# Squares added over chunks on VectorE, and memory keys and values made ahead of their root

## The reference

```
def _rmsnorm(x, g):
    y = x * rsqrt(mean(x * x, axis=-1, keepdims=True) + RMS_EPS)
    return y * g

def _mem_kv(mem, mem_norm_g, w_mem_k, w_mem_v):     # mem (1, 256, 1024)
    m = _rmsnorm(mem, mem_norm_g)
    k = (m @ w_mem_k).reshape(bsz, N_MEM, XA_HEADS, XA_HEAD_DIM)    # 4 heads of 128
    v = (m @ w_mem_v).reshape(bsz, N_MEM, XA_HEADS, XA_HEAD_DIM)
    return k, v

n = _rmsnorm(h, norm1_g)
z = n @ w_in + b_in          # u_s5 | conv_glu_in | q_mem | gate_logits
```

## Time and profile before

| what | value |
|---|---|
| time, median of 3 runs | 1924.89 us (1924.7 to 1926.11) |
| the profiled execution | 1929.2 us |
| its span, first to last instruction | 1927.3 us |
| busy share of the span: PE, DVE, POOL, ACT | 79%, 67%, 33%, 27% |
| HBM read | 665.79 MB |
| mean granted TensorE clock | 0.882 |

### The profile page before, as it was taken

One profiled execution on the slowest core, in us unless ns is written; L12 is line 12 of the kernel. 1 busy time (PEld: TensorE's weight loads), 2 busy tenths in 40 slices (PEclk: granted clock), 3 DMA queues, 4 the chain that ended last, 5 costly groups with the idle time before them and its releaser, 6 DMA issues.

```text
span 1927.3 us, 22321 instructions
## 1 busy us (share of the span) xinstructions
PE 1518.3 (79%) x7779; PEld 788.7 (41%) x7779; DVE 1298.6 (67%) x3346; ACT 526.8 (27%) x1278; POOL 642.6 (33%) x605
## 2 busy tenths in 40 slices
PE   8999999799878998988888889656555776655557
PEld 7888887686433443433333434211111111111113
DVE  5998673327766766676677666776777777777755
ACT  3121142104334343343223233322222121222212
POOL 0020030003444333434344434443434444443442
PEclk9989899899989999999997999777787797777778
DMA  5443463558999999999999999999999999999997
GB/s 211 143 88 110 164 156 113 184 191 326 418 418 385 418 418 418 417 417 414 419 409 409 419 420 420 405 422 417 415 422 418 407 402 422 421 422 422 415 421 285
DMA packets 112706, 675.45 MB, mean 350 GB/s; under 512 B 12784, under 2 KB 15296, under 8 KB 42576
## 3 DMA queue, kind: packets, MB, share of 16 engines
q0 software_dynamic: 80816, 577.23, 73.5%
q1 hardware_dynamic: 31216, 95.87, 14.0%
q10 hardware_dynamic: 560, 0.92, 0.2%
HBM read 665.79 MB, written 6.21 MB: 349 GB/s over the span
## 4 chain that ended last, share of the span: by engine, by line
PE 41%; DMA 41%; issue 8%; DVE 5%; POOL 2%; ACT 2%; ACTq 0%; SPq 0%; POOLq 0%; DVEq 0%
DMA upper<-in_peer_uv,upper 21%; DMA lower<-in_peer_uv,upper 19%; PE pair L1191 11%; PE pair L669 7%; PE pair L680 6%; PE pair L1037 5%; PE pair L783 2%; PE pair L1186 2%; DVE upper L2112 2%; PE pair L983 1%; POOL upper L645 1%; ACT upper L1590 1%; DVE lower L2112 1%; POOL lower L645 1%; PE pair L714 1%
## 5 line engine op out<-in xcount | busy, mean ns | idle before, releaser
L1191 PE MATMUL pair<-upper 64*64 64x512 f32 x2368 | 378.7, 750 | 210.4 <-ACT upper L1590 210.3
L645 POOL DMA_INDIRECT upper<-in_peer_uv,upper x324 | 359.0, 1108 | 504.9 <-PE pair L1191 410.6
L645 POOL DMA_INDIRECT lower<-in_peer_uv,upper x220 | 246.7, 1122 | 487.9 <-PE pair L1191 283.0
L1191 PE MATMUL pair<-lower,upper 64*64 64x512 f32 x1600 | 265.0, 772 | 132.7 <-ACT upper L1590 132.6
L2112 DVE CUSTOM_DVE_ANT_0 upper<-upper 128x1024 f32<-128x1024 f32 x172 | 210.8, 1226 | 123.7 <-DMA upper<-in_peer_uv,upper 123.6
L2112 DVE CUSTOM_DVE_ANT_0 upper<-upper,lower 128x1024 f32<-128x1024 f32 x152 | 186.2, 1225 | 129.8 <-DMA upper<-in_peer_uv,upper 129.4
L1191 PEld LDWEIGHTS pair<-upper 64*64 64x64 f32 x2368 | 89.4, 163 | 406.0 <-ACT upper L1590 279.6
L1590 ACT ACTIVATE upper<-upper 128x64 f32<-128x64 f32 (+2 forms) x543 | 155.4, 338 | 307.4 <-DVE upper L2128 304.9
L1398 ACT ACTIVATE upper<-upper 128x4 f32<-128x4 f32 (+1 forms) x141 | 41.9, 297 | 640.8 <-DVE upper L2112 640.8
L1037 PE MATMUL pair<-lower 128*128 128x288 f32 x704 | 212.5, 432 | 4.2 <-ACT upper L1448 4.2
L2112 DVE CUSTOM_DVE_ANT_0 lower<-lower,upper 128x1024 f32<-128x1024 f32 x116 | 142.1, 1225 | 87.5 <-DMA lower<-in_peer_uv,upper 87.4
(11 more groups left out here) (425 smaller groups left out, 1788.5 us busy)
## 6 DMA issues: line engine op xcount, KB each, us to landing
lower<-in_w_in SPq DMA_DIRECT2D x64, 512.0 KB, 4.8
lower<-in_peer_q SPq DMA_DIRECT2D x28, 512.0 KB, 8.0
lower<-in_proj SPq DMA_DIRECT2D x48, 256.0 KB, 7.2
lower<-in_w_out SPq DMA_DIRECT2D x16, 512.0 KB, 4.7
upper<-in_peer_uv,upper POOLq DMA_INDIRECT x324, 12.4
upper<-in_cache_k SPq DMA_DIRECT2D x8, 512.0 KB, 4.5
upper<-in_cache_v SPq DMA_DIRECT2D x8, 512.0 KB, 4.4
lower<-in_peer_uv,upper POOLq DMA_INDIRECT x220, 12.5
```

The source lines that it names most:

```text
L645: pool.indirect_dma_start(row(g), None, a["peer_uv"], bass.IndirectOffsetOnAxis(ap=idx[:, n % 8, j:j + 1], axis=0)).then_inc(row_in[g % RI ...
L1191: mm = pe.matmul(acc[put, r, :], d[own, 0:64], v[own, h * 512:(h + 1) * 512], start=begun, stop=ended)
```

## The change

The sums of squares move. ScalarE squares as before, but VectorE adds the eight squared chunks into the first, memory then tokens, and counts `sums_ok`; TensorE sums over the partitions with one product by ones per half of the tokens, and one for the memory. A second small product with the operands exchanged gives the memory's sum per memory token as a column (`mcol`), beside the row `mr`.

Keys and values no longer wait for the memory's root. VectorE multiplies the memory by its gain alone, and TensorE begins with the four key blocks. The reciprocal root is multiplied in afterwards: into the keys by VectorE (`kT` times `mr`, four instructions, counted by `key_step`), into the values by ScalarE's copy with a scale per partition (`mcol`), two instructions in place of one. In `JOBS` the keys stand ahead of the two sums, and the tokens' sum ahead of the memory's. On VectorE the token norm comes first, then the reciprocals for the memory and the keys' products, then the S5 discretisation as before. SP loads the constants second, tokens behind the first key block, and the S5 pack behind the second value block.

The diff, without the two definitions of semaphores and `mcol` and without the two places (GpSimd's store of the keys, TensorE ahead of the attention) that now wait for `key_step` instead of the keys' eviction:

```diff
@@ -67,7 +67,7 @@
 
 GATES = [f"G{q}.{b}" for q in range(KD) for b in range(3)]
 PRODUCTS = [f"P{q}.{b}" for q in range(KD) for b in (0, 2)] + [f"P{q}.1" for q in range(KD)]
-JOBS = (["ssm", "ssx"] + [f"k{c}" for c in range(4)] + ["v"]
+JOBS = ([f"k{c}" for c in range(4)] + ["ssx", "ssm", "v"]
         + [f"u{c}" for c in range(4)]
         + ["ag0", "ai0", "ag1", "ai1", "T"] + [f"ET{b}" for b in range(4)]
         + ["ag2", "ai2", "z00", "z01", "z02", "ag3", "z10", "z11", "ai3", "q0", "q1", "q2", "q3"]
...
@@ -460,9 +462,7 @@
         @block.sync
         def _(sp):
             sp.dma_start(memT, a["mem_t"]).then_inc(mem_in, 16)
-            sp.dma_start(nT, a["x_t"]).then_inc(x_in, 16)
             sp.dma_start(const, a["consts"]).then_inc(consts_in, 16)
-            sp.dma_start(s5p, a["s5_pack"]).then_inc(s5_in, 16)
 
             def load(name, src, k=KD):
                 s, n = LOAD[name]
...
@@ -484,8 +484,12 @@
 
             for j in range(4):
                 load(f"k{j}", a["w_mem_k"][j])
+                if j == 0:
+                    sp.dma_start(nT, a["x_t"]).then_inc(x_in, 16)
             for j in range(4):
                 load(f"v{j}", a["w_mem_v"][j])
+                if j == 1:
+                    sp.dma_start(s5p, a["s5_pack"]).then_inc(s5_in, 16)
             sp.dma_start(h0.rearrange("p a b c -> p (a b c)"), a["h0"]).then_inc(h0_in, 16)
             for j in range(4):
                 load(f"u{j}", a["w_in"][j])
...
@@ -572,7 +576,7 @@
             pool.affine_select(out=ident, in_=ident, compare_op=ALU.not_equal, fill=1.0, base=0,
                                pattern=[[-1, P]], channel_multiplier=1).then_inc(made, 1)
             pool.memset(ones, 1.0).then_inc(made, 1)
-            filled(pool, "ssm")
+            pool.wait_ge(sums_ok, 2)
             pool.memset(Tm[:, 0:L - 1], 0.0).then_inc(t_zero, 1)
             filled(pool, "v")
             for j in range(HALF):
...
@@ -692,19 +696,6 @@
 
 
             pe.wait_ge(made, 2)
-            ps = begin("ssm")
-            for k in range(KD):
-                pe.wait_ge(msq_ok, k + 1)
-                mm = pe.matmul(ps[:, 0, 0:MEM], ones, msq[:, k, :], start=(k == 0), stop=(k == KD - 1))
-            mm.then_inc(full[0], 1)
-            ps = begin("ssx")
-            for k in range(KD):
-                pe.wait_ge(xsq_ok, k + 1)
-                for h in range(2):
-                    mm = pe.matmul(ps[:, h, 0:HT], ones, xsq[:, k, h * HT:(h + 1) * HT],
-                                   start=(k == 0), stop=(k == KD - 1))
-            mm.then_inc(full[1], 1)
-
             for j in range(4):
                 w = loaded(f"k{j}")
                 ps = begin(f"k{j}")
...
@@ -713,6 +704,16 @@
                         pe.wait_ge(m_ok, k + 1)
                     mm = pe.matmul(ps[:, 0, 0:MEM], w[:, k, :], memT[:, k, :], start=(k == 0), stop=(k == KD - 1))
                 mm.then_inc(full[JOB[f"k{j}"][0]], 1)
+            ps = begin("ssx")
+            pe.wait_ge(sums_ok, 2)
+            for h in range(2):
+                mm = pe.matmul(ps[:, h, 0:HT], ones, xsq[:, 0, h * HT:(h + 1) * HT], start=True, stop=True)
+            mm.then_inc(full[JOB["ssx"][0]], 1)
+            ps = begin("ssm")
+            pe.matmul(ps[:, 0, 0:MEM], ones, msq[:, 0, :], start=True, stop=True)
+            for m in range(2):
+                mm = pe.matmul(ps[:, 1, 4 * m:4 * m + 4], msq[:, 0, m * P:(m + 1) * P], ones[:, 0:4], start=True, stop=True)
+            mm.then_inc(full[JOB["ssm"][0]], 1)
             ps = begin("v")
             for j in range(4):
                 loaded(f"v{j}")
...
@@ -1204,17 +1206,18 @@
             act.wait_ge(x_in, 16)
             for k in range(KD):
                 act.activation(xsq[:, k, :], nT[:, k, :], ACT.Square).then_inc(xsq_ok, 1)
-
-            emptied(act, "ssm")
-            act.activation(mr, mr, ACT.Sqrt).then_inc(rms_ok, 1)
-            emptied(act, "ssx")
-            act.activation(xr, xr, ACT.Sqrt).then_inc(rms_ok, 1)
-
-            act.wait_ge(s5_in, 16)
-            act.activation(at(tab, G), s5p[:, 0:G], ACT.Tanh, scale=1.0 / 16).then_inc(s5_scan_in, 1)
             for j in range(4):
                 ps = filled(act, f"k{j}")
                 act.activation(kT[:, j, :], ps[:, 0, 0:MEM], ACT.Copy).then_inc(drained(f"k{j}"), 1)
+
+            emptied(act, "ssx")
+            act.activation(xr, xr, ACT.Sqrt).then_inc(rms_ok, 1)
+            emptied(act, "ssm")
+            act.activation(mr, mr, ACT.Sqrt)
+            act.activation(mcol, mcol, ACT.Sqrt).then_inc(rms_ok, 1)
+
+            act.wait_ge(s5_in, 16)
+            act.activation(at(tab, G), s5p[:, 0:G], ACT.Tanh, scale=1.0 / 16).then_inc(s5_scan_in, 1)
             act.wait_ge(epad_ok, 1)
             act.activation(at(tab + 288 * 2, 288), at(tab + 288 * 2, 288), ACT.Tanh, scale=0.5).then_inc(s5_scan_in, 1)
             act.activation(at(tab + 288 * 3, 288), at(tab, 288), ACT.Sin)
...
@@ -1222,7 +1225,9 @@
             act.activation(at(tab + 2304, G), at(tab + 2304, G), ACT.Sin, scale=0.5).then_inc(s5_scan_in, 1)
             act.wait_ge(consts_in, 16)
             ps = filled(act, "v")
-            act.activation(vm.rearrange("p a b -> p (a b)"), flat(ps, 1024), ACT.Copy).then_inc(drained("v"), 1)
+            act.wait_ge(key_step, 1)
+            act.activation(vm[:, 0, :], ps[:, 0, :], ACT.Copy, scale=mcol[:, 0:1])
+            act.activation(vm[:, 1, :], ps[:, 1, :], ACT.Copy, scale=mcol[:, 1:2]).then_inc(drained("v"), 1)
 
             hist = ain[:, :, ARUN:].rearrange("p c (b k) -> p c b k", b=NB)
 
...
@@ -1619,19 +1624,31 @@
 
             tt, ts, stt = dve.tensor_tensor, dve.tensor_scalar, dve.scalar_tensor_tensor
 
+            dve.wait_ge(consts_in, 16)
+            for k in range(KD):
+                dve.wait_ge(msq_ok, k + 1)
+                ts(memT[:, k, :], memT[:, k, :], c("gm", k), None, ALU.mult).then_inc(m_ok, 1)
+            for v, ready in ((msq, msq_ok), (xsq, xsq_ok)):
+                for k in range(1, KD):
+                    dve.wait_ge(ready, k + 1)
+                    link(tt(v[:, 0, :], v[:, 0, :], v[:, k, :], ALU.add))
+                dve.sem_inc(sums_ok, 1)
+            ps = filled(dve, "ssx")
+            ts(halves(xr), two(ps), 1.0 / D, RMS_EPS, ALU.mult, ALU.add).then_inc(drained("ssx"), 1)
             ps = filled(dve, "ssm")
-            ts(mr, ps[:, 0, 0:MEM], 1.0 / D, RMS_EPS, ALU.mult, ALU.add).then_inc(free[0], 1)
-            dve.wait_ge(consts_in, 16)
+            ts(mr, ps[:, 0, 0:MEM], 1.0 / D, RMS_EPS, ALU.mult, ALU.add)
+            ts(mcol, ps[:, 1, 0:8].rearrange("p (m c) -> p m c", m=2)[:, :, 0], 1.0 / D, RMS_EPS, ALU.mult, ALU.add
+               ).then_inc(drained("ssm"), 1)
             dve.wait_ge(rms_ok, 1)
-            link(dve.reciprocal(mr, mr))
-            for k in range(KD):
-                stt(memT[:, k, :], memT[:, k, :], c("gm", k), mr, ALU.mult, ALU.mult).then_inc(m_ok, 1)
-            ps = filled(dve, "ssx")
-            ts(halves(xr), two(ps), 1.0 / D, RMS_EPS, ALU.mult, ALU.add).then_inc(free[1], 1)
-            dve.wait_ge(rms_ok, 2)
             link(dve.reciprocal(xr, xr))
             for k in range(KD):
                 stt(nT[:, k, :], nT[:, k, :], c("g1", k), xr, ALU.mult, ALU.mult).then_inc(n_ok, 1)
+            dve.wait_ge(rms_ok, 2)
+            dve.reciprocal(mcol, mcol).then_inc(key_step, 1)
+            link(dve.reciprocal(mr, mr))
+            for j in range(HEADS):
+                emptied(dve, f"k{j}")
+                tt(kT[:, j, :], kT[:, j, :], mr, ALU.mult).then_inc(key_step, 1)
 
             W = 9 * G
 
```

More of the change, by code:

```diff
@@ L280, in hybrid_step @@
         rcol = at(SM + 600, 2)
+        mcol = at(SM + 634, 2)
         mx_b, nmx_b, asum_b, ars_b = (at(SM + 602 + 8 * i, 4, 2) for i in range(4))
@@ L365, in hybrid_step @@
         msq_ok, xsq_ok, rms_ok, m_ok, n_ok = (sem(n) for n in ("msq_ok", "xsq_ok", "rms_ok", "m_ok", "n_ok"))
+        sums_ok, key_step = sem("squares_added"), sem("memory_keys_scaled")
         epad_ok, s5_scan_in = sem("epad_ok"), sem("s5_functions_ok")
@@ L598, in _ @@
             pool.memset(masked_q, 0.0).then_inc(q_zero, 1)
-            for n in ("k0", "k1", "k2", "k3", "v"):
-                emptied(pool, n)
+            emptied(pool, "v")
+            pool.wait_ge(key_step, 1 + HEADS)
             pool.dma_start(o["mem_k"], kT).then_inc(mem_out, 16)
@@ L772, in _ @@
             gates(0, 1)
-            for n in ("q0", "q1", "q2", "q3", "k0", "k1", "k2", "k3", "v"):
+            for n in ("q0", "q1", "q2", "q3", "v"):
                 emptied(pe, n)
+            pe.wait_ge(key_step, 1 + HEADS)
             def gate_by_gate(lo, hi):
```

## The result

The changed kernel takes 1927.83 us at the median of 12 runs (1925.55 to 1932.09), the kernel before 1924.80 us beside it (1923.37 to 1926.41). The ratio is 1.0016 [1.0009, 1.0024]: **3.0 us slower**, 0.16%. That is inside the 0.2% which the prediction calls no change, but the interval excludes 1, the sign is not the forecast one (1.4 us faster), and the median lies 0.3 us above the range.

The account below looks back on a forecast made before the run. TensorE bounds the start, with VectorE's slack ahead of T at 9.8 us. T starting 3.0 us earlier, less 1.6 for its low clock, gives 1.4 off the 1924.89 median: 1923.5, range 1918.5 to 1927.5.

Parts of the forecast that it names:

- TensorE's gain ahead of T: From the keys to T: TensorE runs 7.3 us earlier and would reach T at 98.8.
- rival (c): Loads at the start: key blocks two to four land at about 20, 4.6 us slower, 1929.5; chance 0.13.
- The S5 chain starts: VectorE ahead of T: token norm and key scaling delay the chain 6.8 us, from 32.76 to 39.6.
- VectorE's second gated product: VectorE behind T: it runs at 110.8, 3.6 us later than before, still leaving slack ahead of the scan.
- (a): At T: the clock holds or falls late in T, 3.0 us earlier, 1921.9; chance 0.15.
- (b): Ahead of T: VectorE isn't late, up to 7.3 us earlier, 1917.6; chance 0.17.
- a shift at T reaches the end: Behind T: the 1.4 us gain passes through scan and gathers to the end, with nothing swallowing it.
- The wait, 5.5 instead of 4.3: TensorE ahead of T: a new wait for VectorE takes 4.3 of the 7.3 us gained.
- Epad at 96.33 + 6.8 = 103.1: VectorE's last S5 product, which T needs, comes 6.8 us later, so T starts at 103.1, 3.0 us earlier.
- T at the low clock, 13.85 instead of 11.6: TensorE in T: after the wait the clock is low and T lasts 11.6 us instead of 9.97, losing 1.6.
- if all 64 instructions of T run at eleven in 2 us: Small products T at the low clock: this assumed pace gives 11.6 us for T.
- ScalarE's issues: Behind T: no term of their own; ScalarE's work starts at T's end, and the next projection waits for it.

Follow-up runs that it names:

- the delayed kernel before: Kernel before the change, with eight products of 128x272 that nothing reads put on TensorE ahead of T: 1928.87 us, ratio 1.0019.
- the later history: Changed kernel with GpSimd's clearing of the pads and loads of the convolution history moved from behind the values to behind the second input projection: 1926.35 us, ratio 1.0001.
- the filled wait: Changed kernel with twelve products that nothing reads on TensorE between the projections and its wait for Epad: 1924.52 us, ratio 0.9993.
- the last version: Changed kernel with part of the S5 chain early, GpSimd's clearing and history loads moved, and ScalarE's seven DMA issues behind its transpose copies: 1915.80 us, ratio 0.9947.

## Why the prediction missed, step by step

**Right, with its numbers.** TensorE's gain ahead of T: values at 26.43 (forecast 26.3), projections at 40.33 (40.1), through at 99.15 (98.8). The keys ended at 24.88 (24.5), so rival (c), late key blocks, did not happen; that the result lies nearer to its 1929.5 than to the forecast is chance, since T started at 104.69 and not at its 109.1. The S5 chain starts at 39.68 (39.6). T waits for VectorE, with the clock at 0.50, and VectorE's second gated product runs at 111.18 (110.8). Rivals (a), a clock that holds, and (b), no wait for VectorE, fell with that. That a shift at T reaches the end, which the forecast claimed, is shown by the delayed kernel before.

**The wait, 5.5 instead of 4.3.** The prediction kept the S5 chain at 63.57 us and moved it. But moved by 6.8 us it meets the history loads that GpSimd issues when the values are done, and four of its instructions take longer, 1.45 us in all. The step that failed is "Epad at 96.33 + 6.8 = 103.1": the 6.8 were right, but the step moved a chain along the time axis without asking what then runs beside it, and the last product came 1.6 us later than that. Shown by the later history, where the 1.45 us are gone.

**T at the low clock, 13.85 instead of 11.6.** This is the largest miss, a mis-sized term: "if all 64 instructions of T run at eleven in 2 us". The mechanism, a wait and then T at the low clock, was right. I took eleven instructions in 2 us as a rate, 0.18 us each. But a stretch counts every instruction that reaches into it, those at its edges as well: after, the three stretches of T count 69 where there are 64. The price is 13.85/64 = 0.216 us, and 64 of those are 2.25 us more than I reckoned. Put in for the 11.6, it turns the forecast of 1.4 us earlier into 0.9 later.

**ScalarE's issues, 0.88 longer.** No term had them: the prediction let ScalarE's work begin at T's end and last as before, without a reason. One of the seven took 1.48 us instead of 0.61. One such issue or two stand in six of the ten kernels (0.81 to 1.48), none in the kernel before, in its delayed form, in the one with the filled wait and in the last version, where the issues come later. I did not find what sets them apart; GpSimd's DMAs beside them are not enough, since the filled wait has them too, and SyncE issued nothing beside the long one of the changed kernel (none of its issues from 115 to 130). This stays open.

**The sum.** Forecast at the next projection: -3.0 for T's start, +1.6 for T. Measured: -1.44, +3.88 and +0.88. The three misses are 1.6, 2.3 and 0.9 us, all in one direction, 4.7 together, and the change of the medians missed by 4.4 (3.0 later for 1.4 earlier). The range failed because its upper end held no miss of the low-clock price, though that price rested on one count. Of the 3.3 us at the next projection the wait and the clock are shown by experiments; for the issues only the place and the size are known.

**Which rule would have told.** The Trainium skill, "TensorE: Matmul & The Clock Gate", section "Part 1: The HAM clock gate", says that the throttled rate is the default and that activity releases it. The forecast read from this that a wait ahead of T speaks against the change, and the trace agrees: 0.50 through the whole of T. On the chain, the Trainium skill, "SBUF — State Buffer", section "Who interferes with whom", says that a VectorE instruction in a two-port mode, which tensor_scalar can enter and tensor_tensor cannot, contends with GpSimd for a port pair: the one that issues first holds it for the whole instruction, and the other blocks. The trace agrees: 0.18 became 3.09 beside a 3.08 us clearing that began 0.03 us ahead of it, while the TENSOR_TENSORs beside GpSimd's issues kept their 0.19.

## What to carry to other kernels

When work is taken off one engine and another thereby becomes late at a junction, the loss isn't only the wait: price what the waiting engine does *afterwards* at its low clock, and by a duration per instruction, not by a count in a stretch. When a chain is moved in time, look at what will run beside it at its new place, on GpSimd above all. And take the remedy from the same place: here VectorE's list ahead of T had idle time at the start, and filling it turned a loss of 3 us into a gain of 6. The version with GpSimd and ScalarE's issues moved as well stands at 9, but the medians do not tell these later steps apart one by one.

## What the hardware showed that I had not expected

- **A short VectorE instruction can stand for a whole GpSimd one**: TENSOR_SCALAR of 128x32, 0.18 us alone, took 3.09 beside a memset of 3.08, and up to 0.63 beside GpSimd's DMA issues.
- **Useless work can pay**: twelve products that nobody reads kept the grant at 1.00 into T, and T took 9.49 us instead of 13.84.
- **The same T took 8.41 to 13.84 us** over the kernels, by where in it the clock fell. The kernel before has it fall inside T as well, without a wait.
- **A DMA issue on ScalarE**, 0.61 us as a rule, took up to 1.48 us. The cause is open.
